# Ten modulation units of the first block's projection, multiplied and added on VectorE instead of on the array

## The chip, the cores and the metric

One core of a Trainium2 chip runs the whole kernel. The metric is the device time of one execution in microseconds (us). The engines are PE (TensorE, the matmul array; PEld is its weight load), DVE (VectorE), ACT (ScalarE), POOL (GpSimd) and SP, which issues the transfers. Each has its own instruction queue and goes through it in order. An engine waits for another by a semaphore, and whatever stands behind the waiting instruction in the same queue waits with it.

## The reference

A first block (a state-space scan, windowed attention, a mixture of experts) is followed by two layers of a second block. The change touches only how the modulation vectors are made while the first block's input is projected. They are one row times a matrix, for the latent tokens and for the context:

```python
mod_x = jax.nn.silu(c) @ w_ada[layer] + b_ada[layer]
mod_c = jax.nn.silu(c_ctx) @ w_ada[layer] + b_ada[layer]
sh1, sc1, g1, sh2, sc2, g2 = jnp.split(mod_x[:, None, :], 6, axis=-1)
...
hx = rms_norm(x, norm1[layer]) * (1 + sc1) + sh1
hc = rms_norm(ctx, norm1[layer]) * (1 + csc1) + csh1
zx, xbc_x, dt_x, qx, kx, vx = split_projection(hx @ w_in[layer])
zc, xbc_c, dt_c, qc, kc, vc = split_projection(hc @ w_in[layer])
```

`w_ada` has 1024 rows and 6 x 1024 columns, `c` and `c_ctx` are vectors of 1024, and all is float32. Inside the stretch looked at here the modulation only has to be ready for later phases; the projection itself does not read it.

## The kernel before

All weights come through one stream: units of 1024 rows by 256 columns (1 MB), loaded by SP in a fixed order into a ring of four slots (`weight_ring`). A slot is loaded again when the unit in it has been used. A matmul tells this: `retire()` marks the units held so far as used, and the next matmul that passes through `note()` carries the signal (`WeightStream`, line 75).

The first projection is `seven_phase` with the name `project1` (called at line 3357). It has nine weight units, numbered 0 to 8 here, and behind each stand two modulation units in the stream (`burst=2`), 18 in all, numbered 0 to 17. Modulation units 8 to 17 stand behind the last five weight units. A weight unit is a matrix product in seven block products instead of eight (a Strassen form): POOL makes four sums of the quarters of the weights (`weight_quarters`, 128x512 each, during the unit before), DVE has made the sums of the columns once at the start, PE makes seven products of four matmuls (128x256), ACT copies three of the results out of PSUM, POOL makes one small sum (`m15`), and DVE makes four sums, called here u2, c22, c12 and c21 by their semaphores. Units 0, 1, 2 and 8 also have context columns, 16 more matmuls ahead of the seven products. Behind the four sums of units 0 to 3 DVE also does the short convolution of that unit's output (`ShortConv.taps`).

A modulation unit has four steps, each with a counter of its own, all in class `Modulation` (line 290):

- `rows`, on PE at the end of a weight unit: eight matmuls (32 columns of `silu_c` against 128x256 of the weights), which leave partial rows in PSUM;
- `copy`, on ACT: those rows to SBUF;
- `turn`, on PE, behind the first and the second product of the next weight unit: two small matmuls that turn the rows into columns and add them;
- `add`, on DVE: the bias. It stands in DVE's queue behind the four sums of its unit, so ahead of the next unit's u2.

Two later phases, `gates` and `mlp`, use the other form, `SummedModulation` (line 370), with the same four steps and one more, `piece`, on DVE. There DVE multiplies the weights by the values of `silu_c`, one value for each partition, and adds the eight row blocks up in `mod_products`, once for the latent vector and once for the context's. A piece is four instructions of 128x256, so a modulation unit is four pieces, 16 instructions: two `tensor_scalar` (line 403) and 14 `scalar_tensor_tensor` (line 406). `rows` then waits until the unit's 16 instructions are done (line 421), and needs four matmuls of 128x128 that only add over the partitions. `turn` is one matmul. A unit named in `whole` takes the old form in every step.

PE's queue is the order of the calls in the Python loop: the products of unit i, then `rows` of its two modulation units, then unit i+1. DVE's queue in the same way: u2, c22, c12, c21, taps, two `add`, then unit i+1.

Of the kernel before, what the change touches and what calls it, by code (L numbers as in the profile page):

```python
# [2833 lines left out]
def seven_phase(core, name, b, lo, n, units, th=None, conv=None, mods=(), burst=0, heads=None, tail=None):  # L2834
# [6 lines left out]
    q = Quarters  # L2841
    U = len(units)
    with core.phase(name, U + len(mods)) as ph:
        bg = Modulation(core, ph, mods) if mods else None
        kq = KeyQuery(core, ph, *heads) if heads else None
        st = SquareTail(core, ph, *tail) if tail else None
        if th is None:
# [17 lines left out]
        def quarter(i, r, c):  # L2865
            return units[i][r][:, T - 2 * n + c * n:T - 2 * n + (c + 1) * n]
# [126 lines left out]
        def _(dve):  # L2993
            link = chain(dve, vec_link) if conv else None

            def plus(dst, bank, other, f):
                if f == 1.0:
                    return nc.vector.tensor_tensor(dst, bank, other, ALU.add)  # L2998
                return nc.vector.scalar_tensor_tensor(dst, bank, f, other, ALU.mult, ALU.add)

            column_quarters(nc.vector, b, lo, n, th, t_ready, False)
            for i in range(U):
# [7 lines left out]
                dve.wait_ge(products, 7 * i + 3)  # L3010
                dve.wait_ge(m1_out, i + 1)
                plus(quarter(i, 0, 1), y, quarter(i, 1, 0), f).then_inc(u2_out, 1)
                if kq and len(kq.turns.get(i, ())) == 2:
                    kq.sines(dve, stream.tables_loaded, i, 0)
                    kq.add(dve, i, 0)
                dve.wait_ge(products, 7 * i + 5)
                dve.wait_ge(m15_out, i + 1)
                plus(quarter(i, 1, 1), y, quarter(i, 1, 1), f).then_inc(c22_out, 1)
                if kq and len(kq.turns.get(i, ())) == 1:
                    kq.sines(dve, stream.tables_loaded, i, 0)  # L3020
                    kq.add(dve, i, 0)
                dve.wait_ge(products, 7 * i + 6)
                dve.wait_ge(u2_out, i + 1)
                plus(quarter(i, 0, 1), z, quarter(i, 0, 1), f).then_inc(c12_out, 1)
                dve.wait_ge(products, 7 * i + 7)
                plus(quarter(i, 1, 0), y, quarter(i, 1, 0), f).then_inc(c21_out, 1)
                if kq:
                    kq.sines(dve, stream.tables_loaded, i, 1)
                if conv and i < conv.pairs:
# [773 lines left out]
```

## Time and profile before

| | us |
|---|---|
| median of 3 runs | 4199.21 (4193.64 to 4199.97) |
| the profiled execution | 4195.06 |
| its span, first to last instruction | 4193.2 |
| PE busy | 3856.6 (92% of the span) |
| DVE busy | 1874.2 (45%) |
| POOL busy | 1031.2 (25%) |
| ACT busy | 873.3 (21%) |
| granted PE clock, mean | 0.967 of full |

The phase `project1` lies from 75.8 to 249.1 us of the span; its last five weight units run from 159.6 to 241.7 us. In the tables a busy share is a share of time in which the engine had an instruction under way; a matmul row of the timeline with "x8" is four matmuls of float32, each shown as two passes. The granted clock is 1.00 at 2.4 GHz and 0.50 at 1.2 GHz.

### The profile page before, as it was taken

The numbers are of one execution on the slowest core, as the hardware profiler recorded it, in microseconds if no ns is written. First come the engines' busy times: TensorE is split into PE (matmuls) and PEld (weight loads), VectorE is DVE, ScalarE is ACT, GpSimd is POOL, SyncE is SP. The second block draws the span as 40 slices with busy tenths as digits, with TensorE's granted clock in tenths as the row PEclk, the third lists the DMA queues.
The fourth block names the chain that finished last, engine by engine and source line by source line (L and its number), as shares of the span: only waits on it lengthen the run. The fifth ranks groups of instructions, "written<-read, shape, count | busy, mean of one in ns | idle before, by whom it ended". The sixth has DMA issues, their size and how long they took to land. (4 is left out here: it accounts for less than half of the span.)

```text
span 4193.2 us, 47533 instructions
## 1 busy us (share of the span) xinstructions
PE 3856.6 (92%) x18216; PEld 2581.9 (62%) x18216; DVE 1874.2 (45%) x3401; ACT 873.3 (21%) x1681; POOL 1031.2 (25%) x862
## 2 busy tenths in 40 slices
PE   6967969999989988999997999999899989989998
PEld 4865734444465566555554555555787657758887
DVE  3445332222322266588543666645225645234344
ACT  2122321111111265111213000001123511220001
POOL 1301200000014211223341322231142023434443
PEclk8978989999999999999998999999999999999999
DMA  5410159999811100122221223221110012222221
GB/s 197 171 73 16 49 237 390 394 395 395 340 36 50 46 11 1 62 91 98 76 98 40 101 101 121 101 91 51 45 61 31 1 67 83 74 81 72 90 82 60
DMA packets 72155, 479.61 MB, mean 114 GB/s; under 512 B 8256, under 2 KB 9664, under 8 KB 18176
## 3 DMA queue, kind: packets, MB, share of 16 engines
q1 hardware_dynamic: 68720, 465.86, 29.4%
q0 software_dynamic: 2640, 8.65, 0.7%
q8 instruction: 147, 2.41, 0.2%
q10 hardware_dynamic: 576, 2.10, 0.1%
q14 instruction: 72, 0.59, 0.0%
HBM read 472.39 MB, written 4.19 MB: 114 GB/s over the span
## 5 line engine op out<-in xcount | busy, mean ns | idle before, releaser
L2164 DVE SCALAR_TENSOR_TENSOR sb_x_all<-ps,sb_modulation_ada,sb_x_all 128x512 f32<-128x512 f32 x144 | 106.5, 750 | 323.4 <-PE ps L2001 302.9
L754 PE MATMUL ps<-projected,weight_ring 128*128 128x384 f32 (+1 forms) x672 | 245.8, 521 | 0.0
L754 PEld LDWEIGHTS ps<-projected,weight_ring 128*128 128x128 f32 x672 | 127.7, 190 | 106.1 <-issue 45.9
L3116 PE MATMUL ps<-h2b,weight_ring 128*128 128x384 f32 (+1 forms) x512 | 154.1, 445 | 23.6 <-PEq L246 23.6
L1151 DVE TENSOR_REDUCE attention_shift<-ps 128x1 f32<-128x768 f32 (+1 forms) x160 | 130.9, 845 | 74.8 <-PE ps L1039 74.3
L2554 DVE SCALAR_TENSOR_TENSOR projected<-projected,sb_vectors 128x497 f32<-128x497 f32 (+26 forms) x270 | 157.8, 649 | 1.6
L1039 PE MATMUL ps<-projected 64*128 64x256 f32 (+1 forms) x576 | 133.8, 519 | 24.9 <-DVE projected L1180 15.0
L406 DVE SCALAR_TENSOR_TENSOR mlp_mod_products<-weight_ring,sb_silu_c,mlp_mod_products 128x256 f32<-128x256 f32 x280 | 154.6, 622 | 0.1
L2414 PE MATMUL ps<-projected,gates_weight_sums 128*128 128x384 f32 (+1 forms) x512 | 149.6, 435 | 5.0 <-POOL gates_weight_sums L2694 5.0
L1837 POOL DMA_INDIRECT h<-tokens,own_tokens x31 | 31.1, 1002 | 491.2 <-PE ps L1972 416.4
L2414 PE MATMUL ps<-h2b,weight_ring 128*128 128x384 f32 (+1 forms) x512 | 150.1, 436 | 1.9 <-PEq L246 1.9
L2414 PE MATMUL ps<-h2b,gates_weight_sums 128*128 128x384 f32 (+1 forms) x512 | 149.7, 435 | 0.6 <-POOL gates_weight_sums L2691 0.4
L3095 POOL TENSOR_TENSOR mlp_weight_sums<-weight_ring 128x512 f32<-128x512 f32 x32 | 45.8, 1432 | 398.3 <-DMA weight_ring<-w_stream 315.2
L2998 DVE TENSOR_TENSOR projected<-ps,projected 128x384 f32<-128x384 f32 (+1 forms) x72 | 35.3, 490 | 233.7 <-PE ps L2903 233.7
L3116 PEld LDWEIGHTS ps<-h2b,weight_ring 128*128 128x128 f32 x512 | 98.3, 194 | 66.1 <-issue 29.4
L1988 PE MATMUL ps<-expert_weights,experts_x_turned 128*64 128x256 f32 x944 | 135.0, 384 | 1.9 <-DVE experts_x_turned L2156 1.9
L1112 ACT ACTIVATE attention_prob<-ps,attention_shift 128x768 f32<-128x768 f32 (+1 forms) x160 | 129.6, 813 | 34.1 <-DVE attention_shift L1151 33.2
L2394 POOL TENSOR_TENSOR merged<-merged,gates_sigmoid 128x768 f32<-128x768 f32 (+1 forms) x44 | 67.2, 1538 | 278.4 <-DVE gates_sigmoid L2620 278.4
L2001 PE MATMUL ps<-experts_slot_owner,experts_down_out_pair 128*128 128x512 f32 x240 | 134.0, 643 | 0.0
L796 PE MATMUL ps<-weight_ring,h2b 128*128 128x256 f32 (+1 forms) x576 | 108.6, 352 | 20.9 <-PEq L246 20.9
L2414 PEld LDWEIGHTS ps<-projected,gates_weight_sums 128*128 128x128 f32 x512 | 97.8, 191 | 47.2 <-POOL gates_weight_sums L2694 6.1
L2063 PE MATMUL ps<-expert_weights,experts_hidden_turned 128*64 128x512 f32 x528 | 120.6, 597 | 6.2 <-DMA expert_weights<-w_moe 3.4
(673 smaller groups left out, 8023.9 us busy)
## 6 DMA issues: line engine op xcount, KB each, us to landing
weight_ring<-w_stream SPq DMA_DIRECT2D x218, 1024.0 KB, 5.0
expert_weights<-w_moe SPq DMA_DIRECT2D x125, 1024.0 KB, 21.8
weight_ring<-w_moe SPq DMA_DIRECT2D x40, 1024.0 KB, 24.0
h2b<-w_moe SPq DMA_DIRECT2D x33, 1024.0 KB, 21.4
weight_ring<-w_stream SPq DMA_DIRECT2D x16, 512.0 KB, 3.6
weight_ring<-w_stream SPq DMA_DIRECT2D x16, 384.0 KB, 3.2
sb_x_all<-xT SPq DMA_DIRECT2D x1, 3072.0 KB, 11.7
tokens<-h_tokens ACTq DMA_DIRECT2D x4, 512.0 KB, 12.5
```

The lines of the kernel that those rows point to most:

```text
L406: ins = self.core.nc.vector.scalar_tensor_tensor(acc, w[:, k, :], c, acc, ALU.mult, ALU.add)
L754: ins = nc.tensor.matmul(core.ps[:, 2 * slot + half, 0:n], w_of(k), h_of(k)[:, a:a + n], start=(first and k == 0), stop=(last and k == chu ...
L796: ins = nc.tensor.matmul(core.ps[:, 2 * (j % 4), 0:n], h[:, k, t * P:(t + 1) * P], w[:, k, c:c + n], start=(k == 0), stop=(k == KD - 1))
L1039: ins = nc.tensor.matmul(scores(p, i)[:, at:at + n], q, k[:, c:c + n], start=True, stop=True, skip_group_check=True)
L1112: nc.scalar.activation(prob[:, b, 0:n], scores(p, i)[:, 0:n], ACT.Exp, bias=shift[:, b:b + 1], accum_out=sums[:, b:b + 1]).then_inc(p_read ...
L1151: nc.vector.tensor_reduce(shift[:, b:b + 1], scores(p, i)[:, 0:columns(p)], AX.X, ALU.max, negate=True).then_inc(peak_ready, 1)
L1988: ins = nc.tensor.matmul(out[OWN * j:OWN * (j + 1), :], x_t[:, k, :], w[j][:, k, :], start=(k == 0), stop=(k == KD - 1), skip_group_check= ...
L2001: nc.tensor.matmul(ps[:, bank, :], y_pair[:, m % 2, r, k % 4 * P:(k % 4 + 1) * P], owner[:, r, :], start=True, stop=True).then_inc(spread_ ...
L2063: ins = nc.tensor.matmul(down[OWN * r:OWN * (r + 1), :], hid_t[:, k % 2, OWN * (k // 2):OWN * (k // 2 + 1)], w[j][:, k, :], start=(k == 0) ...
L2414: ins = nc.tensor.matmul(acc, wq[:, k, :], bq[:, k, :], start=(first and k == 0), stop=(last and k == 3), skip_group_check=True)
L2554: ins = nc.vector.scalar_tensor_tensor(pr[:, acc + c, lo:hi], pr[:, val + c, lo + d:hi + d], w, pr[:, acc + c, lo:hi], ALU.mult, ALU.add)
L3116: ins = nc.tensor.matmul(acc, wq[:, k, :], bq[:, k, :], start=(first and k == 0), stop=(last and k == 3), skip_group_check=True)
```

## The change

In a `seven_phase` that has a convolution, which is `project1` alone, the modulation is of the summed form. `whole` is the first `burst * conv.pairs` = 8 modulation units, which keep the array form. Modulation units 8 to 17, behind weight units 4 to 8, are summed. Behind each of DVE's four sums stand two calls of `piece`; for the units in `whole` they only count. The other phases that call `seven_phase` are as before. The extra tile `mod_products` takes 4 KB of each partition.

```diff
-        bg = Modulation(core, ph, mods) if mods else None
+        summed = conv is not None
+        whole = range(burst * conv.pairs) if conv else ()
+        bg = SummedModulation(core, ph, mods, lambda i: i + i // burst + 1, whole) if summed else \
+            Modulation(core, ph, mods) if mods else None
...
                 plus(quarter(i, 0, 1), y, quarter(i, 1, 0), f).then_inc(u2_out, 1)
+                if summed:
+                    for _ in range(burst):
+                        bg.piece(dve)
...
                 plus(quarter(i, 1, 1), y, quarter(i, 1, 1), f).then_inc(c22_out, 1)
+                if summed:
+                    for _ in range(burst):
+                        bg.piece(dve)
...
                 plus(quarter(i, 0, 1), z, quarter(i, 0, 1), f).then_inc(c12_out, 1)
+                if summed:
+                    for _ in range(burst):
+                        bg.piece(dve)
...
                 plus(quarter(i, 1, 0), y, quarter(i, 1, 0), f).then_inc(c21_out, 1)
+                if summed:
+                    for _ in range(burst):
+                        bg.piece(dve)
```

What `bg` calls now for modulation units 8 to 17 (in the kernel before, used by other phases):

```python
    def piece(self, dve):
        n, q = divmod(self.n_piece, 4)
        ...
        if n in self.whole:
            return
        if q == 0 and n >= self.turns:
            dve.wait_ge(self.rows_done, n - self.turns + 1)
        w = self.core.stream.arrived(dve, self.place(n))
        ...
                if k == 0:
                    ins = self.core.nc.vector.tensor_scalar(acc, w[:, k, :], c, None, ALU.mult)
                else:
                    dve.wait_ge(self.multiplied, self.done_to(n) + 2 * k + s - 1)
                    ins = self.core.nc.vector.scalar_tensor_tensor(acc, w[:, k, :], c, acc, ALU.mult, ALU.add)

    def rows(self, pe):
        ...
        stream.take(pe)
        if n >= self.turns:
            pe.wait_ge(self.added, n - self.turns + 1)
        pe.wait_ge(self.multiplied, self.done_to(n + 1))
        stream.retire()
        for j in range(4):
            s, m = divmod(j, 2)
            ins = nc.tensor.matmul(self.bank(n)[32 * j:32 * j + 32, 0:P], self.core.first_of_32(),
                                   self.acc[:, n % self.turns, s, m * P:(m + 1) * P], start=True, stop=True,
                                   skip_group_check=True)
```

DVE's queue from the end of unit 3 to the first `add` of unit 5, before (`z_q` is written by the four sums, lines 364 and 464 are `add`):

```order
L1247 SCALAR_TENSOR_TENSOR conv_out<-conv_in,sb_vectors,conv_out 128x510 x2
L364 TENSOR_TENSOR sb_modulation_ada<-ps,sb_vectors 128x4 x2
L2998 TENSOR_TENSOR z_q<-ps,z_q 128x256 x4
L364 TENSOR_TENSOR sb_modulation_ada<-ps,sb_vectors 128x4 x2
L2998 TENSOR_TENSOR z_q<-ps,z_q 128x256 x4
```

The same place now (the line of the sum, 2998 before, is 3001):

```order
L364 TENSOR_TENSOR sb_modulation_ada<-ps,sb_vectors 128x4 x2
L3001 TENSOR_TENSOR z_q<-ps,z_q 128x256
L403 TENSOR_SCALAR project_mod_products<-weight_ring,sb_silu_c 128x256 x2
L406 SCALAR_TENSOR_TENSOR project_mod_products<-weight_ring,sb_silu_c,project_mod_products 128x256 x6
L3001 TENSOR_TENSOR z_q<-ps,z_q 128x256
L406 SCALAR_TENSOR_TENSOR project_mod_products<-weight_ring,sb_silu_c,project_mod_products 128x256 x8
L3001 TENSOR_TENSOR z_q<-ps,z_q 128x256
L403 TENSOR_SCALAR project_mod_products<-weight_ring,sb_silu_c 128x256 x2
L406 SCALAR_TENSOR_TENSOR project_mod_products<-weight_ring,sb_silu_c,project_mod_products 128x256 x6
L3001 TENSOR_TENSOR z_q<-ps,z_q 128x256
L406 SCALAR_TENSOR_TENSOR project_mod_products<-weight_ring,sb_silu_c,project_mod_products 128x256 x8
L464 TENSOR_TENSOR sb_modulation_ada<-ps,sb_vectors 128x4 x2
```

Thirty-two instructions have come in between a unit's sums and behind the last of them, eight after each.

PE's queue from the last product of unit 4 into unit 5, with the semaphores that are waited for, before:

```order
L2903 MATMUL ps<-mixed,weight_ring 128x256 x3
L317 MATMUL ps<-weight_ring,sb_silu_c 32x256 [waits project1_mod_added,unit_loaded2]
L317 MATMUL ps<-weight_ring,sb_silu_c 32x256 x7
L317 MATMUL ps<-weight_ring,sb_silu_c 32x256 [waits project1_mod_added,unit_loaded3]
L317 MATMUL ps<-weight_ring,sb_silu_c 32x256 x7
L2903 MATMUL ps<-h,weight_ring 128x256 [waits project1_c11_out,unit_loaded0]
```

and now:

```order
L2906 MATMUL ps<-mixed,weight_ring 128x256 x3
L423 MATMUL ps<-project_mod_products,sb_constants 32x128 [waits project1_mod_added,project1_mod_multiplied,unit_loaded2]
L423 MATMUL ps<-project_mod_products,sb_constants 32x128 x3
L423 MATMUL ps<-project_mod_products,sb_constants 32x128 [waits project1_mod_multiplied,project1_mod_added,unit_loaded3]
L423 MATMUL ps<-project_mod_products,sb_constants 32x128 x3
L2906 MATMUL ps<-h,weight_ring 128x256 [waits project1_c11_out,unit_loaded0]
```

The number of matmuls falls from 16 to 8, each of its two groups now also waits for DVE's counter of finished multiplications, and the next unit's first product stands behind both groups as it did.

## Rows read from the trace of the kernel before

**Rows 1.** Windows, all engines: us, length, busy (instructions) each, clock, DMA
```profile
174.60:189.70 15.10, 15.10 (x101) 12.42 (x97) 2.02 (x6) 1.92 (x5) 5.75 (x5) 1.00 0.55 211
...
219.70:243.00 23.30, 23.18 (x140) 19.51 (x136) 2.26 (x8) 3.72 (x9) 0.72 (x1) 1.00 0.38 147
```

**Rows 2.** Timeline of PE, units 6 to 8: start, length, what
```profile
189.67 1.99 PE L2903 MATMUL ps<-h,weight_ring 128*128 128x256 f32 x8
191.50 0.50 PE L341 MATMUL ps<-sb_constants,project_mod_rows 128*128 128x2 f32 x4
...
202.85 1.93 PE L317 MATMUL ps<-weight_ring,sb_silu_c 128*32 128x256 f32 x32
204.71 1.99 PE L2903 MATMUL ps<-h,weight_ring 128*128 128x256 f32 x8
...
219.76 7.17 PE L2913 MATMUL ps<-h,weight_ring 128*128 128x256 f32 x32
```

**Rows 3.** Timeline of DVE, the four sums of units 4, 6, 8
```profile
165.97 0.42 DVE L2998 TENSOR_TENSOR z_q<-ps,z_q 128x256 f32<-128x256 f32 x1 [0.21 <-PE ps L2903]
...
196.05 0.42 DVE L2999 SCALAR_TENSOR_TENSOR z_q<-ps,z_q 128x256 f32<-128x256 f32 x1 [1.67 <-PE ps L2903]
...
233.04 0.42 DVE L2998 TENSOR_TENSOR k_twice<-ps,k_twice 128x256 f32<-128x256 f32 x1 [1.67 <-PE ps L2903]
```

**Rows 4.** Timeline of ACT at the end of this phase
```profile
241.84 0.38 ACT L331 ACTIVATE project_mod_rows<-ps 128x256 f32<-128x256 f32 x1 [0.48 <-PE ps L317]
...
249.34 1.28 ACT L1312 ACT_TABLE_LOAD   x1 [0.26 <-PEq L246]
```

**Rows 5.** Timeline of DVE in the mlp phase, the pieces there
```profile
2406.68 0.61 DVE L403 TENSOR_SCALAR mlp_mod_products<-weight_ring,sb_silu_c 128x256 f32<-128x256 f32 x2
2407.21 4.48 DVE L406 SCALAR_TENSOR_TENSOR mlp_mod_products<-weight_ring,sb_silu_c,mlp_mod_products 128x256 f32<-128x256 f32 x6
...
2417.02 0.56 DVE L3236 TENSOR_TENSOR mlp_u<-ps,mlp_m 128x384 f32<-128x384 f32 x1 [2.02 <-PE ps L3116]
2417.49 3.25 DVE L406 SCALAR_TENSOR_TENSOR mlp_mod_products<-weight_ring,sb_silu_c,mlp_mod_products 128x256 f32<-128x256 f32 x8
2420.66 0.55 DVE L3251 TENSOR_TENSOR down<-mlp_u,mlp_m 128x384 f32<-128x384 f32 x1
```

**Rows 6.** Timeline of POOL in the mlp phase, same stretch
```profile
2408.60 1.39 POOL L3095 TENSOR_TENSOR mlp_weight_sums<-weight_ring 128x512 f32<-128x512 f32 x1 [15.69 <-DMA weight_ring<-w_stream]
2409.96 1.45 POOL L3096 TENSOR_TENSOR mlp_weight_sums<-weight_ring 128x512 f32<-128x512 f32 x1
```

**Rows 7.** Timeline of POOL, weight sums during unit 4
```profile
168.44 1.26 POOL L2691 TENSOR_TENSOR project_weight_sums<-weight_ring 128x512 f32<-128x512 f32 x1 [3.38 <-DMA weight_ring<-w_stream]
...
172.24 1.27 POOL L2696 TENSOR_TENSOR project_weight_sums<-weight_ring,project_weight_sums 128x512 f32<-128x512 f32 x1
```

**Rows 8.** DMA issues from 159.6 to 243 us
```profile
weight_ring<-w_stream SPq DMA_DIRECT2D x15, 1024.0 KB, 6.8
```

**Rows 9.** Timeline of PE in the mlp phase: the summed form
```profile
2403.24 0.43 PE L423 MATMUL ps<-mlp_mod_products,sb_constants 128*32 128x128 f32 x8
...
2406.28 0.28 PE L450 MATMUL ps<-sb_constants,mlp_mod_rows 128*128 128x4 f32 x2
```

**Rows 10.** Timeline of PE: work after three gaps
```profile
152.35 1.99 PE L2903 MATMUL ps<-mixed,project_weight_sums 128*128 128x256 f32 x8 [2.94 <-DVE conv_in L2998]
...
277.00 9.28 PE L1408 MATMUL ps<-state_x,b_tokens 128*128 128x256 f32 x32 [7.17 <-PEq L246]
...
309.65 0.69 PE L1491 MATMUL ps<-ssd_scan_segment,dt_x 128*64 128x128 f32 x2 [3.67 <-DVE ssd_scan_segment L1539]
```

**Rows 11.** Windows around those gaps, columns as in rows 1
```profile
149.40:152.40 3.00, 0.06 (x2) 0.05 (x1) 2.89 (x6) 0.39 (x1) 2.38 (x2) 1.00 0.00 0
277.00:280.90 3.90, 3.90 (x9) 3.17 (x10) 0.73 (x2) 0.00 (x0) 0.00 (x0) 0.50 0.02 4
...
309.70:315.00 5.30, 5.30 (x25) 5.30 (x26) 2.14 (x6) 1.12 (x2) 0.00 (x0) 0.50 0.02 3
```

## The prediction

> **What bounds the kernel now.** I read the windows of the last weight units first, then the timelines of PE and DVE there, then the phase that already has the summed form. The windows show PE busy for all of unit 5, 15.10 of 15.10 us, at the full clock, while DVE is busy 2.02 us and POOL 5.75 us; the window of unit 8 with what follows reads the same way, 23.18 of 23.30 us [rows 1]. So PE bounds this stretch, and work taken from it would shorten the kernel one for one, if nothing else came late. A unit without context takes 15.04 us (204.71 - 189.67), of which the two modulation units' array work is 1.86 us (204.71 - 202.85) [rows 2]. The one thing PE hands to others and gets back late enough to matter is small: the first of DVE's four sums starts 6.38 us into unit 6 (196.05 - 189.67) [rows 2, 3].
>
> **What the change takes from PE.** `rows` of a pair falls from 1.86 us to about 0.8: the summed form's group of one modulation unit is 0.43 us [rows 2, 9]. A `turn` falls from 0.50 to 0.28 us, 0.44 for two [rows 2, 9]. That is some 1.5 us a unit and 7.5 us over five units, if PE never had to wait.
>
> **What it gives to DVE.** Thirty-two instructions a unit. In the mlp phase eight multiply-adds in a row start 3.17 us before what follows them (2420.66 - 2417.49), 0.396 each, and two `tensor_scalar` take 0.53 (2407.21 - 2406.68) [rows 5]. A sum of 384 columns there holds the queue for 0.47 us (2417.49 - 2417.02) with a duration of 0.56; the sums here have 256 columns and a duration of 0.42, so I take 0.33 [rows 3, 5]. From the start of u2 to the last multiply-add's end: 4 x 0.33 + 2 x (0.53 + 6 x 0.396) + 2 x 3.17 + 0.08 for the last one's tail = 13.55 us, without any stall.
>
> **Why that lies on the path.** It cannot run beside the whole unit. u2 is ahead of every piece of its unit, and u2 needs the unit's third product; the first product in turn stands in PE's queue behind the second `rows` group of the unit before, which now waits for the last piece of that unit. And the queue of DVE has the two `add` ahead of u2, which wait for `turn` in the same new unit, so DVE cannot begin the next unit's pieces early either. The chain closes: start of the unit, three products and two turns, u2, eight pieces of four instructions, `rows`, next unit. Between u2 and the end of unit 6's products PE has only 202.85 - 196.05 = 6.8 us of work [rows 2, 3], and the pieces with the sums take twice that. What PE waits for last at the end of each of the five units is DVE.
>
> c22 comes later too, since two pieces, eight instructions, stand ahead of it, and the seventh product waits for it. That moves PE's work within the gap and costs nothing at the end. The first modulation unit's `rows` is ready after four pieces, in the gap as well.
>
> **Two surcharges.** First, POOL's four weight sums for the next unit. In the mlp phase the six multiply-adds that meet two of POOL's sums take 4.48 us where 6 x 0.396 + 0.08 = 2.46 are due, 1.0 us for each sum that they meet, and POOL's sums themselves take 1.39 and 1.45 us [rows 5, 6] where they take 1.26 and 1.27 alone [rows 7]. In unit 4 all four lie behind u2 (168.44 to 173.51, u2 at 165.97) [rows 3, 7], so 4.0 us. In units 5 to 7 the slot for the next weight unit comes free with the second `rows` group, its load is then alone, and the median of a load here, three at a time, is 6.8 us [rows 8]; POOL should start some 5 to 8 us into the unit, about when u2 does. I take 3.5 us, between 0 and the 4.0 of all four. Unit 8 has no unit behind it: 0.
>
> The Trainium skill (SBUF — State Buffer, Who interferes with whom) says that a VectorE instruction with two inputs in SBUF and a GpSimd instruction that reads SBUF exclude each other for a whole instruction, and the second to issue fully blocks. By that rule four sums of 1.27 us could hold DVE for 5.1 us instead of 3.5 to 4.0, and my sum would be up to 6 us longer. The rows above have 1.0 us each, and the sum goes by them.
>
> Second, PE's clock. PE will stand for some 6 us at the end of each of these units. After a gap of 2.94 us the clock is still 1.00, after 3.67 and 7.17 us work starts again at 0.50, and stays there for 5.3 and 3.9 us [rows 10, 11]. Half of that time is lost, 2.0 to 2.7 us, all of it ahead of u2. I take 2.2 us a unit for units 5 to 8; bounds 0 (no fall) and 5.9 (half speed all the way to u2 doubles the 5.94 us before it). Unit 4 starts with the clock full.
>
> The Trainium skill (TensorE: Matmul & The Clock Gate, HAM oscillation) describes this: a loop that leaves PE idle once in every round restarts cold in every round. By a rule that a warm PE stays warm the sum would be 8.8 us shorter; the gaps in this trace bear the page out.
>
> **The sum.** Unit 4, whose turns are still of the old form: 6.38 + 13.55 + 4.0 + 0.4 for the waking of PE and the second `rows` = 24.3, against 15.04: +9.3. Units 5 to 7: 6.38 - 0.44 = 5.94, + 2.2 + 13.55 + 3.5 + 0.4 = 25.6: +10.55 each, 31.7 for three. Unit 8 has context first: u2 starts at 13.28 (233.04 - 219.76), less 0.44, + 2.2 + 13.55 + 0.4 + 0.1 = 29.1 until ACT's last copy, which was at 241.84 - 219.76 = 22.08: +7.0 [rows 2 to 4]. ACT has the convolution's silu behind that copy and ends the phase, so the phase ends later by the whole shift: its next phase began at 249.34 [rows 4]. Nothing that follows waits for anything but this phase's end, so I let nothing of it come back.
>
> Sum: 9.3 + 31.7 + 7.0 = 48.0 us. The profiled execution took 4195.06 us, so 4243 us by it; it lies 4.15 us below the median of the runs, and against the median this is 4247 us, my forecast. What tells from no change here is 0.2%, 8.4 us.
>
> **The rivals.**
>
> The other side: DVE is hidden, PE bounds as before, and only the 7.5 us of saved array work count: 4192 us. For it: DVE is nearly empty here, 2.02 us of 15.10 [rows 1]. Against: the pieces start only behind the third product, and are 32. It decides where the 32 instructions and the four sums fit into 6.8 us: (6.8 - 4 x 0.33) / 32 = 0.17 us an instruction, against 0.396. Chance 2%.
>
> PE's clock does not fall in the gaps, since each has a small group of matmuls in it: the sum loses 4 x 2.2 = 8.8 us, 4238 us. For it: 2.94 us did no harm. Against: between the first group and the last piece lie four pieces and two sums, over 6 us. 11%.
>
> POOL does not hold DVE up, since its sums fall ahead of u2 (the load comes alone and early): 4.0 + 3 x 3.5 = 14.5 us less, 4233 us. It needs POOL to be through 6 us into the unit, and its load then must land before the unit begins. 7%. With both of these, 48.0 - 8.8 - 14.5 = 24.7 us are left: 4224 us, 2%.
>
> The clock stays low until u2 in every unit, the bound of 5.9 us: 4 x 3.7 = 14.8 us more, 4262 us. The longest stretch at 0.50 in the rows is 5.3 us, so this needs a worse restart than they show. 8%.
>
> That the change does not do what it says: the order of the queues shows the 160 instructions in place and 80 array matmuls replaced by 40. I give that nothing of its own.
>
> **How the numbers follow.** The forecast has 69%, with a range of its own of 4240 to 4254 us (clock 2.0 to 2.7 a unit, POOL 2.5 to 4.0). For 8 times in 10 I take 4231 to 4260: it takes in the case without POOL's delay, the one with the clock full, and most of the slow one. The first rival's 4192 lies 0.17% below the median, on the edge, so its 2% and 1% for what I have not thought of are split: faster by over 0.2% 1%, within 0.2% 2%. Slower: 97%.
>
> **What would show it.** Windows of units 4 to 8: PE busy about 13 us of a unit of 24 to 26 us, DVE about 18. PE's idle time there put down to DVE `project_mod_products`, some 6 to 8 us a unit, five times. The clock at 0.50 at the start of units 5 to 8 and at 1.00 when the unit's fifth product runs. DVE's multiply-adds at a start distance of 0.40 us, but three or four of some 1.45 us behind u2. The next phase's table load at about 297 us instead of 249.34. I am wrong if a unit stays at 15 us or less, if PE's wait is for a load or for POOL, or if a later phase changes by more than 3 us.

## The result, and the profile after

Before: 4196.43 us median of 4 runs beside the new ones (4191.75 to 4199.97). After: 4245.27 us median of 4 (4241.65 to 4248.90). The ratio is 1.0116, 95% interval 1.0102 to 1.0129: slower by 48.8 us, where 4247 was forecast.

The profiled execution of after took 4246.2 us, at a mean clock of 0.962 (0.967 before). Its page begins with these busy times. DVE had 1874.2 us in 3401 instructions before, so the 160 new ones are all there; PE had 3856.6 us, and is no less busy although it has less to do, since part of its work now runs at half the clock (the windows below show it):

```profile
span 4244.3 us, 47539 instructions
PE 3861.7 (91%) x18116; PEld 2586.9 (61%) x18116; DVE 1947.8 (46%) x3561; ACT 871.4 (21%) x1681; POOL 1031.1 (24%) x862
```

The windows of the five changed units, from one first product to the next, the last one up to ACT's last copy (columns as in [rows 1]), answer to the two windows there:

```profile
157.58:181.96 24.38, 14.53 (x85) 11.79 (x81) 23.33 (x46) 1.81 (x5) 6.26 (x5) 0.89 0.53 212
181.96:207.72 25.76, 16.58 (x81) 13.20 (x77) 16.92 (x38) 1.70 (x5) 5.84 (x5) 0.83 0.34 123
207.72:232.57 24.85, 15.66 (x81) 12.48 (x77) 16.93 (x38) 1.71 (x5) 5.85 (x5) 0.84 0.35 122
232.57:258.62 26.05, 16.87 (x81) 13.37 (x77) 16.92 (x38) 1.71 (x5) 5.85 (x5) 0.83 0.34 126
258.62:288.10 29.48, 22.85 (x114) 19.15 (x110) 13.96 (x38) 2.63 (x8) 0.72 (x1) 0.85 0.30 107
```

Units 4 to 7, which took 15.04 us, take 24.4 to 26.1. PE is busy for 14.5 to 16.9 us of it, DVE for 16.9 (23.3 in unit 4, which has the convolution too). The clock, 1.00 before, is 0.83 to 0.89 in the five windows. The timeline of PE through unit 5, answering to [rows 2] and [rows 9], shows where it stands:

```profile
181.37 0.65 PE L423 MATMUL ps<-project_mod_products,sb_constants 128*32 128x128 f32 x8 [6.30 <-DVE project_mod_products L406]
181.96 3.78 PE L2906 MATMUL ps<-h,weight_ring 128*128 128x256 f32 x8
...
185.82 2.58 PE L2906 MATMUL ps<-h,project_weight_sums 128*128 128x256 f32 x8
...
197.14 1.99 PE L2906 MATMUL ps<-mixed,weight_ring 128*128 128x256 f32 x8 [1.61 <-DVE z_q L3001]
200.40 0.42 PE L423 MATMUL ps<-project_mod_products,sb_constants 128*32 128x128 f32 x8 [1.26 <-DVE project_mod_products L406]
207.13 0.66 PE L423 MATMUL ps<-project_mod_products,sb_constants 128*32 128x128 f32 x8 [6.31 <-DVE project_mod_products L406]
207.72 3.58 PE L2906 MATMUL ps<-h,weight_ring 128*128 128x256 f32 x8
```

Three gaps: 1.61 us for c22, which stands behind the first eight instructions of DVE; 1.26 us for the first modulation unit's pieces; 6.31 us for the second's. Behind the long one the first product (x8) takes 3.78 us instead of 1.99, at a granted clock of 0.50 (181.96 to 185.80). The waits from 157 to 295 us put the summing matmuls' part down in one line (waited for: total, times, longest):

```profile
PE ps L423 <- DVE project_mod_products L406: 38.6, 10, 6.3
```

DVE through the same unit answers to [rows 3] and [rows 5], and POOL to [rows 6] and [rows 7]:

```profile
190.39 0.42 DVE L3001 TENSOR_TENSOR z_q<-ps,z_q 128x256 f32<-128x256 f32 x1 [1.67 <-PE ps L2906]
190.73 1.62 DVE L403 TENSOR_SCALAR project_mod_products<-weight_ring,sb_silu_c 128x256 f32<-128x256 f32 x2
192.27 4.48 DVE L406 SCALAR_TENSOR_TENSOR project_mod_products<-weight_ring,sb_silu_c,project_mod_products 128x256 f32<-128x256 f32 x6
196.67 0.41 DVE L3001 TENSOR_TENSOR z_q<-ps,z_q 128x256 f32<-128x256 f32 x1
197.01 3.24 DVE L406 SCALAR_TENSOR_TENSOR project_mod_products<-weight_ring,sb_silu_c,project_mod_products 128x256 f32<-128x256 f32 x8
...
203.74 3.25 DVE L406 SCALAR_TENSOR_TENSOR project_mod_products<-weight_ring,sb_silu_c,project_mod_products 128x256 f32<-128x256 f32 x8
```

```profile
189.65 1.27 POOL L2691 TENSOR_TENSOR project_weight_sums<-weight_ring 128x512 f32<-128x512 f32 x1
190.87 1.33 POOL L2692 TENSOR_TENSOR project_weight_sums<-weight_ring 128x512 f32<-128x512 f32 x1
192.16 1.32 POOL L2694 TENSOR_TENSOR project_weight_sums<-project_weight_sums,weight_ring 128x512 f32<-128x512 f32 x1
193.55 1.33 POOL L2696 TENSOR_TENSOR project_weight_sums<-weight_ring,project_weight_sums 128x512 f32<-128x512 f32 x1
```

DVE works without a pause from u2 at 190.39 to 206.99, and its first two groups, which lie beside POOL's last three sums, are long by about 3 us. ACT's end of the phase answers to [rows 4]:

```profile
287.83 0.28 ACT L439 ACTIVATE project_mod_rows<-ps 128x128 f32<-128x128 f32 x1 [6.68 <-PE ps L423]
...
295.22 1.28 ACT L1312 ACT_TABLE_LOAD   x1 [0.26 <-PEq L246]
```

I measure the phase from unit 4's first product to this load, so that small differences ahead of it don't count: 249.34 - 159.59 = 89.75 us before, 295.22 - 157.58 = 137.64 after, 47.9 us more. This is called the phase's shift below.

### The profile page after: what moved, and what is told of

Same layout as the page of the kernel before. It is cut to its first block and busy times, and to the rows that moved or that the text cites. A ratio compares the mean times of both kernels' runs of the same rounds, so it can differ in the third digit from the quotient of the medians.

```text
span 4244.3 us, 47539 instructions
## 1 busy us (share of the span) xinstructions
PE 3861.7 (91%) x18116; PEld 2586.9 (61%) x18116; DVE 1947.8 (46%) x3561; ACT 871.4 (21%) x1681; POOL 1031.1 (24%) x862
## 5 line engine op out<-in xcount | busy, mean ns | idle before, releaser
L754 PEld LDWEIGHTS ps<-projected,weight_ring 128*128 128x128 f32 x672 | 127.7, 190 | 106.1 <-issue 45.9
L1039 PE MATMUL ps<-projected 64*128 64x256 f32 (+1 forms) x576 | 134.5, 521 | 25.5 <-DVE projected L1180 15.1
L3131 PEld LDWEIGHTS ps<-h2b,weight_ring 128*128 128x128 f32 x512 | 98.1, 194 | 65.9 <-issue 29.1
## 6 DMA issues: line engine op xcount, KB each, us to landing
h2b<-w_moe SPq DMA_DIRECT2D x33, 1024.0 KB, 21.5
```

The lines of the kernel that those rows point to most:

```text
L754: ins = nc.tensor.matmul(core.ps[:, 2 * slot + half, 0:n], w_of(k), h_of(k)[:, a:a + n], start=(first and k == 0), stop=(last and k == chu ...
L1039: ins = nc.tensor.matmul(scores(p, i)[:, at:at + n], q, k[:, c:c + n], start=True, stop=True, skip_group_check=True)
L3131: ins = nc.tensor.matmul(acc, wq[:, k, :], bq[:, k, :], start=(first and k == 0), stop=(last and k == 3), skip_group_check=True)
```

## The experiments

All medians are of 4 to 11 runs, each beside runs of the kernel before on the same chip: 4194.85 us for the first four, 4194.5 for the next four, 4196.64 for the last two. "A unit" is unit 5, 6 or 7.

### What the shift is made of

Three kernels took one surcharge, the other, or both away. First POOL's: its four weight sums stay in the queue but work on 8 columns instead of 512, so that the products of these units are not the reference's (e5_pool):

```diff
-def weight_quarters(pool, s, w, ready, i):
+def weight_quarters(pool, s, w, ready, i, narrow=False):
...
+    if narrow:
+        for j in range(4):
+            pool.tensor_tensor(s[:, j, 0:1, 0:8], w[:, 0:1, 0:8], w[:, 4:5, 0:8], ALU.add).then_inc(ready, 1)
+        return
...
-                weight_quarters(pool, sw[:, i % 2], w, s_ready, i)
+                weight_quarters(pool, sw[:, i % 2], w, s_ready, i, conv is not None and i >= 5)
```

> The changed kernel, but POOL's four weight sums of units 5 to 8 work on 8 columns instead of 512, so these units' products are not the reference's. In the changed kernel's trace four of DVE's instructions in unit 4 and three in each of units 5 to 7 take about 1.0 us longer while POOL's sums run, 12.7 us together. Theory: these lie on the chain one for one, and the kernel is 12 to 14 us faster than the changed one, 36 us slower than before. Rival (the stalls are taken in a stretch that something else covers, or the clock's grid eats them): under 5 us faster than the changed one.

Measured: 4230.0 us, ratio 1.0083 [1.0069, 1.0097]; the phase's shift is 36.1 us, 11.8 less than in after. In DVE's timeline the same two groups are now short:

```profile
187.54 0.43 DVE L3005 TENSOR_TENSOR z_q<-ps,z_q 128x256 f32<-128x256 f32 x1 [1.67 <-PE ps L2910]
187.88 0.61 DVE L403 TENSOR_SCALAR project_mod_products<-weight_ring,sb_silu_c 128x256 f32<-128x256 f32 x2
188.40 2.46 DVE L406 SCALAR_TENSOR_TENSOR project_mod_products<-weight_ring,sb_silu_c,project_mod_products 128x256 f32<-128x256 f32 x6
```

The `tensor_scalar` pair goes from 1.62 to 0.61 us and the six multiply-adds from 4.48 to 2.46, one microsecond for each of three instructions. So POOL's sums cost 11.8 us in all; the gap of 6.31 us, which lies behind the collisions, is as it was.

With PE kept busy in the gap by 12 matmuls of no use (e6_filler):

```diff
+FILL = 12
...
-                for _ in range(burst):
+                for r in range(burst):
...
+                    if conv and 4 <= i < 8 and r == 0:
+                        pe.wait_ge(c11_out, i)
+                        for j in range(FILL):
+                            nc.tensor.matmul(banks(i + 1)[0], core.ones[:, :], b[:, 0, 0:256], start=True, stop=True,
+                                             skip_group_check=True)
```

> The changed kernel with 12 matmuls of 128x256 that nobody reads, put on PE behind the first of the two rows groups of units 4 to 7, some 5 us of work in a gap of 6.3. Theory: the clock stays full through the gaps, the three products ahead of u2 take 5.94 us again in units 5 to 8 instead of 7.5 to 8.7, and 8.6 us come back: 40 us slower than before. In the trace the granted clock is 1.00 at the start of units 5 to 8. Rival (the slow restart is not due to the gap, or the fillers run into the last piece and hold the next unit up): as slow as the changed kernel, 48 us, or slower.

Measured: 4231.55 us, ratio 1.0086 [1.0072, 1.0099]; shift 39.1 us, 8.8 less than in after. PE's timeline shows that the restart is at full speed (1.99 us for the first product, and a granted clock of 1.00 at the start of units 5 to 8) although DVE is no earlier:

```profile
198.96 0.43 PE L424 MATMUL ps<-project_mod_products,sb_constants 128*32 128x128 f32 x8 [1.26 <-DVE project_mod_products L407]
199.31 5.45 PE L2967 MATMUL ps<-h,sb_ones 128*128 128x256 f32 x24
205.69 0.43 PE L424 MATMUL ps<-project_mod_products,sb_constants 128*32 128x128 f32 x8 [0.93 <-DVE project_mod_products L407]
```

In unit 4 the clock fell all the same, behind a gap of 2.95 us and the first summing group. There the 12 matmuls themselves took 7.13 us instead of 5.45, at a mean clock of 0.76, and unit 5 began some 0.5 us later than in after:

```profile
175.59 7.13 PE L2967 MATMUL ps<-h,sb_ones 128*128 128x256 f32 x24
```

Both edits together (e7_both; the diffs are the two above):

> Both of these: POOL's weight sums of units 5 to 8 on 8 columns and the 12 matmuls in each gap. Theory: the two surcharges are separate and add up, 21.3 us less than the changed kernel, 27.5 us slower than before; what is left is 32 instructions of DVE a unit in the chain. Rival (they overlap, since what PE loses at the start moves POOL's sums off the pieces): less than 17 us less than the changed kernel.

Measured: 4221.42 us, ratio 1.0062 [1.0049, 1.0076]; shift 26.4 us, 21.5 less than in after, against 11.8 + 8.8 = 20.6 for the two alone. In the phase the surcharges add up. The medians bear this out only roughly: against the kernels before beside them the three lie 35.5, 37.1 and 26.9 us up, so 13.3, 11.8 and 21.9 less than after's 48.8. What is left, 26 us over five units, is that DVE's own run of 13.8 us stands where PE has 6.8 us of work.

Only the last unit's pair summed (e4_last), where neither POOL nor a next unit is behind it:

```diff
-        whole = range(burst * conv.pairs) if conv else ()
+        whole = range(16) if conv else ()
```

> The changed kernel with the first 16 modulation units in the array form, so that only the two behind unit 8 are summed. No POOL sums and a full clock there: 13.28 + 13.55 + 0.4 + 0.1 = 27.3 us to ACT's last copy against 22.08: 5.3 us slower than before. Rival (the loss of a unit is mostly a disturbance that a first summed unit starts, or lies in the changed start of the phase): under 2 us or over 9 us.

Measured: 4204.77 us, ratio 1.0026 [1.0015, 1.0037]; shift 5.7 us, where 5.3 was expected. The median lies 9.9 us above before's, which taken alone is the rival's figure (over 9). In the profile the rest, 3.8 us, comes up between this phase's end and the end of the experts' phase, in code that is the same. So the phase bears the theory out; what makes the rest is not shown.

### Is it the wait, or DVE's work as such?

The array does the rows as in the kernel before, DVE does the 160 instructions at the same places on other data, and PE waits for none of them (e1_nowait):

```diff
-        bg = SummedModulation(core, ph, mods, lambda i: i + i // burst + 1, whole) if summed else \
-            Modulation(core, ph, mods) if mods else None
+        bg = Modulation(core, ph, mods) if mods else None
...
+            def aside(dve):
...
+                            ins = nc.vector.tensor_scalar(acc, b[:, k, 0:UCOLS], c, None, ALU.mult)
...
+                            ins = nc.vector.scalar_tensor_tensor(acc, b[:, k, 0:UCOLS], c, acc, ALU.mult, ALU.add)
...
-                        bg.piece(dve)
+                        aside(dve)
```

> All 18 modulation units are of the array form again, and PE waits for no piece; DVE still does the same 160 multiply-adds in the same places, on columns of h instead of the ring's weights, into a tile that nobody reads. Theory (the loss is the closed chain: PE's rows wait for the last piece, and the next unit's u2 waits for PE): DVE then runs on its own at 13.55 + 0.2 + about 3.5 us for POOL = 17.2 us a unit against PE's 15.04, catches up in unit 8 where PE has 7 us of context work, and the kernel is 1 to 5 us slower than before, not 48. Rival (the pieces cost by being in DVE's queue, because u2 and c22 come late for PE's fifth and seventh product): 30 us or more slower.

Measured: 4206.33 us, ratio 1.0032 [1.0020, 1.0044]; shift 10.6 us. The theory is the nearer, 37 of 47.9 us go with the wait for the pieces, but both missed the size. The 10.6 us that stay are the rival's mechanism, u2 and c22 coming late, at a third of the size that it was given. With no wait to hold the units back, DVE needs more than a unit's time and its sums u2 and c22 come late; twice in unit 6 that stops PE:

```profile
198.37 1.89 PE L2922 MATMUL ps<-h,weight_ring 128*128 128x256 f32 x8
202.43 3.06 PE L2922 MATMUL ps<-mixed,project_weight_sums 128*128 128x256 f32 x8 [2.17 <-DVE z_q L3018]
205.29 2.55 PE L2922 MATMUL ps<-h,project_weight_sums 128*128 128x256 f32 x8
209.75 3.55 PE L2922 MATMUL ps<-mixed,weight_ring 128*128 128x256 f32 x8 [1.91 <-DVE z_q L3018]
```

Two gaps of about 2 us, 5 us apart, and the groups behind them take 3.06 and 3.55 us instead of 1.99: the clock fell here too. That unit took 23.0 us, units 4, 5 and 7 about 16.

### Is DVE too slow, or in the wrong place?

Half of the row blocks (e3_half), the others left out of the computation:

```diff
-            for s in range(2):
+            for s in range(2) if not (self.half and k % 2) else ():
...
```

> As the changed kernel, but only every second row block is multiplied and added, 8 instructions for a modulation unit instead of 16, so half of the sum is left out. Theory: a unit's chain loses 6.3 us. Unit 4: 6.38 + 7.2 + 3.5 + 0.4 = 17.5 us; units 5 to 7: 5.94 + 7.2 + 3.0 + 0.4 = 16.5 us if the clock holds in a gap of some 3 us, 18.7 if not; unit 8 about 1 us less than before. Together 6 us slower than before with the clock full, 13 with a fallen one. Rival (a cost for each unit that does not go with DVE's work, from waits and restarts): half of the loss of 48.8 us or more stays, 24 us slower.

Measured: 4214.44 us, ratio 1.0046 [1.0033, 1.0059]; shift 17.4 us. PE still waits 2.9 to 3.1 us for the last piece in units 4 to 7, and restarts on a lowered clock; I had expected 13 with the clock fallen, and the rival 24, so the median, 19.6 us up, meets neither. Unit 8, expected 1 us shorter than before, has 1.9 us of waiting for its last piece. Halving the work took 30 of the 48 us, not all.

Fourteen of the sixteen instructions of a modulation unit on 8 columns instead of 256 (e2_tiny), which leaves the rest of the columns out:

```diff
+                wk = w[:, k, :]
+                if self.narrow and k:
+                    acc, wk = acc[:, 0:8], w[:, k, 0:8]
...
-                    ins = self.core.nc.vector.scalar_tensor_tensor(acc, w[:, k, :], c, acc, ALU.mult, ALU.add)
+                    ins = self.core.nc.vector.scalar_tensor_tensor(acc, wk, c, acc, ALU.mult, ALU.add)
```

> As the changed kernel, but of each modulation unit's 16 instructions the 14 multiply-adds work on 8 columns instead of 256, so the modulation of these ten units is not computed. DVE then needs about 5 us a unit behind u2, under the 6.8 us that PE has there. Theory: PE never waits, and what is left is the saved array work, 1.5 us a unit, so 5 to 8 us less than before (about 4189). Rival (PE waits for something else that the new form brings, such as the ring's slots that are given back later, or the semaphores of 32 instructions): not faster than before.

Measured: 4224.25 us, ratio 1.0071 [1.0052, 1.0091], of which some 16 us arise in the experts' phase, whose routing hangs on the values: POOL gathers three of the extra blocks of tokens there (`experts_block_index`) instead of two. The phase itself is longer by 15.1 us. This missed by its sign: I had expected 5 to 8 us less than before. The two timelines of the same stretch, DVE's and then PE's, show why:

```profile
190.08 0.42 DVE L3006 TENSOR_TENSOR z_q<-ps,z_q 128x256 f32<-128x256 f32 x1
190.41 0.61 DVE L406 TENSOR_SCALAR project_mod_products<-weight_ring,sb_silu_c 128x256 f32<-128x256 f32 x2
190.94 0.96 DVE L409 SCALAR_TENSOR_TENSOR project_mod_products<-weight_ring,sb_silu_c,project_mod_products 128x8 f32<-128x8 f32 x6
191.82 0.42 DVE L3006 TENSOR_TENSOR z_q<-ps,z_q 128x256 f32<-128x256 f32 x1
192.15 1.23 DVE L409 SCALAR_TENSOR_TENSOR project_mod_products<-weight_ring,sb_silu_c,project_mod_products 128x8 f32<-128x8 f32 x8
```

```profile
189.06 2.00 PE L2911 MATMUL ps<-mixed,weight_ring 128*128 128x256 f32 x8 [0.38 <-DVE z_q L3006]
190.99 0.43 PE L426 MATMUL ps<-project_mod_products,sb_constants 128*32 128x128 f32 x8
193.53 0.54 PE L426 MATMUL ps<-project_mod_products,sb_constants 128*32 128x128 f32 x8 [2.11 <-DVE project_mod_products L409]
193.99 3.53 PE L2911 MATMUL ps<-h,weight_ring 128*128 128x256 f32 x8
```

The last eight instructions stand in DVE's queue behind c21 (191.82), and c21 waits for the unit's seventh product, whose matmuls end at about 191. However short they are, they come after PE has run out of products. Behind the 2.11 us of waiting the clock is down, 3.53 us for the next product. One unit later a wait of the same length left it at 1.00:

```profile
211.87 0.42 PE L426 MATMUL ps<-project_mod_products,sb_constants 128*32 128x128 f32 x8 [2.12 <-DVE project_mod_products L409]
212.23 2.00 PE L2911 MATMUL ps<-h,weight_ring 128*128 128x256 f32 x8
```

The place is not all of it, for the short instructions are short only away from POOL. Beside its sums six of them take three times as long:

```profile
185.69 2.98 DVE L409 SCALAR_TENSOR_TENSOR project_mod_products<-weight_ring,sb_silu_c,project_mod_products 128x8 f32<-128x8 f32 x6
```

That moves c22, c12 and c21 back as well. In unit 8, where POOL has no sums, PE waits 1.41 us for the last pieces; in units 4 to 7 it waits 2.1 to 2.8.

To test that it is the place, only the first row block was kept (e9_first): two `tensor_scalar` a modulation unit, those of the pair's second one behind c12, and nothing behind c21.

```diff
-        self.n_piece = 0
+        self.n_piece, self.per = 0, 16
...
-        return 16 * sum(i not in self.whole for i in range(n))
+        return self.per * sum(i not in self.whole for i in range(n))
...
-        for k in (2 * q, 2 * q + 1):
+        for k in (2 * q, 2 * q + 1) if self.per == 16 else (0,) if q == 0 else ():
...
+        if summed:
+            bg.per = 2
```

> Edit: of the eight row blocks of an image's modulation row only the first is multiplied (two tensor_scalar instructions a unit instead of two and fourteen multiply-adds); the other seven are left out, so the modulation of the layer is not computed, and the later phases, whose routing of tokens to experts hangs on it, may take another time. The phase alone is read: from unit 4's start to the next phase's table load. Theory (what is left of the cost in the two short-instruction runs is the place of the last pieces, not their speed: they stand behind the multilayer perceptron's c12 and c21 of the unit before, and any piece that is long past product 6 is late): one tensor_scalar of 0.26 us behind c12 is finished before TensorE's seventh product of 1.99 us ends, so TensorE waits for no piece, its clock stays at 1.00, and each of five units is shorter by the 1.5 us that TensorE no longer works: the table load comes 7 us earlier than in the kernel before, counted from unit 4's start (5 to 8). Rival (the rows of the modulation unit wait for something else as well, the transfer of the next unit or the rows of ScalarE): gaps of over 1 us before the second group of summing matmuls stay and the table load comes at the same time or up to 10 us later.

(Its c12 and c21 are those of this phase; no multilayer perceptron is near.) Measured: the phase is 6.3 us shorter than before (83.44 against 89.75), inside the 5 to 8 expected; PE waits for a piece 0.23 to 0.36 us in units 4 to 7, and the clock is 1.00 for the five units:

```profile
181.69 0.43 PE L423 MATMUL ps<-project_mod_products,sb_constants 128*32 128x128 f32 x8
182.35 0.43 PE L423 MATMUL ps<-project_mod_products,sb_constants 128*32 128x128 f32 x8 [0.23 <-DVE project_mod_products L403]
182.71 1.99 PE L2908 MATMUL ps<-h,weight_ring 128*128 128x256 f32 x8
```

(The whole kernel is at 4210.9 us, 1.0040 [1.0026, 1.0054]: the experts' phase again, some 19 us longer than before in the profile, with three gathered blocks instead of two as in e2_tiny.) So the array's saving is real, 7.5 us less the small waits, and in this order of the queues it is to be had only by work that is done before the seventh product ends. How much work that may be is not measured: this edit took away three things at once, the instructions behind c21, most of the work, and all but one of a unit's meetings with POOL's sums. That one makes the small wait: the second `tensor_scalar` behind c12 takes 1.36 us beside POOL.

### Can it be made to fit?

The first unit of each pair only, its pieces at the end of the unit before, behind u2 and behind c22 (e8_mix):

```diff
-        whole = range(burst * conv.pairs) if conv else ()
+        whole = [m for m in range(len(mods)) if m < burst * conv.pairs or m % 2] if conv else ()
...
+                if summed and 4 <= i < U - 1:
+                    for _ in range(2):
+                        bg.piece(dve)
...
```

> Only the first modulation unit of each pair behind units 4 to 8 is summed, and its four pieces stand earlier: two ahead of the two adds and u2 (in unit 4 behind u2), one behind u2, one behind c22. Its weights land 3.6 us into the unit. Theory: the last piece is done when the unit's products are, at about 13 us, and each of the five units saves 0.5 us in rows and 0.22 in one turn: 3 to 4 us faster than before, under what this measurement can tell from nothing, but PE's idle time in front of rows shows it in the trace. Rival (POOL's sums and the late u2 push the last piece behind the products): 1 to 3 us of wait in each unit, 4 to 12 us slower than before.

Measured: 4204.43 us, ratio 1.0021 [1.0012, 1.0030]; shift 9.2 us. The rival was right: PE waits for a piece 3.8 us in unit 4, 1.1 to 1.9 in units 5 to 7, and not at all in unit 8. Its timeline of DVE shows two things that I had not reckoned with:

```profile
186.02 4.07 DVE L406 SCALAR_TENSOR_TENSOR project_mod_products<-weight_ring,sb_silu_c,project_mod_products 128x256 f32<-128x256 f32 x4
...
195.44 0.62 DVE L403 TENSOR_SCALAR project_mod_products<-weight_ring,sb_silu_c 128x256 f32<-128x256 f32 x2 [4.68 <-DMA weight_ring<-w_stream]
```

The last four multiply-adds, 1.6 us alone, take 4.07 beside POOL's sums, and the early ones wait for their own weights' transfer. The version mended for both, with POOL's sums of units 6 to 8 held back until the pieces are done, and four modulation units summed instead of five (e10_fit):

```diff
-        whole = range(burst * conv.pairs) if conv else ()
+        whole = [m for m in range(len(mods)) if m < 10 or m % 2] if conv else ()
...
+                if summed and i >= 6:
+                    pool.wait_ge(bg.multiplied, 16 * (i - 5))
...
+                if summed and 4 <= i < U - 1:
+                    for _ in range(2):
+                        bg.piece(dve)
...
```

> Edit: only the modulation units behind units 5 to 8 that come first in their pair are summed (four of ten), their sixteen instructions stand in four pieces: two at the end of the unit before, one behind u2 and one behind c22, and GpSimd's weight sums of units 6 to 8 wait until that unit's pieces are done; the other six go through TensorE as in the kernel before. All of the computation is there. Theory: VectorE has 6.4 us of such work a unit, in places where it waits for TensorE now, no piece meets a weight sum of GpSimd, the last piece is finished some 1.5 us before TensorE's products end, and TensorE saves 0.72 us in each of four units: 4 x 0.72 = 2.9 us less than before, 4192, which is within what can't be told from no change; the phase is 3 us shorter in the profile and its clock stays at 1.00. Rival (VectorE's order has no free place at all: a piece moves c21, c22 or the weight sums that the next unit waits for): TensorE waits 1 to 2.5 us in each of the four units, and the time is 4 to 10 us longer than before.

Measured: 4194.97 us against 4196.64, ratio 0.9997 [0.9988, 1.0006]; the phase is 1.9 us shorter. The summing matmuls wait for nothing:

```profile
193.50 1.99 PE L2908 MATMUL ps<-mixed,project_weight_sums 128*128 128x256 f32 x8 [0.32 <-DVE z_q L3004]
...
198.88 0.43 PE L423 MATMUL ps<-project_mod_products,sb_constants 128*32 128x128 f32 x8
199.12 1.05 PE L317 MATMUL ps<-weight_ring,sb_silu_c 128*32 128x256 f32 x16
```

Most of the 2.9 us hoped for shows in the phase, the rest went to waits of 0.3 to 0.4 us for u2 in units 6 and 7, and none of it can be told from no change in the runs. Ahead of such a u2 one piece still meets a sum of POOL, the small `m15`, and its group takes 2.93 us instead of 2.46:

```profile
190.05 2.93 DVE L406 SCALAR_TENSOR_TENSOR project_mod_products<-weight_ring,sb_silu_c,project_mod_products 128x256 f32<-128x256 f32 x6
```

No version beat the kernel before.

## Why the prediction was right, step by step

**The chain.** Right. Each unit is the sum of three stretches that can be read from the rows above; for unit 5 they are 190.39 - 181.96 = 8.43 to u2, 206.99 - 190.39 = 16.60 of DVE, and 207.72 - 206.99 = 0.73 to the next unit, 25.76 in all. e5_pool's unit, without collisions, has DVE's run at 13.77 us, so 2.83 of the 16.60 are POOL's. The same reading of all five units, forecast beside measured:

| term, us | forecast | measured |
|---|---|---|
| clock, units 5 to 8 | 4 x 2.2 = 8.8 | 2.49, 1.57, 2.78, 1.73 = 8.6 |
| DVE from u2 to the last piece, alone | 13.55 | 13.77 (five times: +1.1) |
| POOL's surcharge, units 4 and 5 to 7 | 4.0 + 3 x 3.5 = 14.5 | 3.5 + 3 x 2.83 = 12.0 |
| from the last piece to the next unit or ACT's copy | 4 x 0.4 + 0.5 = 2.1 | 4 x 0.73 + 0.86 = 3.8 |
| unit 4, 5, 6, 7, 8 to the copy | 24.3, 25.6, 25.6, 25.6, 29.1 | 24.38, 25.76, 24.85, 26.05, 29.21 |
| shift of the phase | 48.0 | 47.9 |

That the shift is within 0.1 us is partly luck: three terms were off by +1.1, -2.5 and +1.7 us and cancel. The forecast of 4247 stood on a median before of 4199.21 us; beside the new runs it was 4196.43, and the two medians lie 48.8 us apart where the sum says 48.0. The range was wider than was said: the chances of the forecast, of the full clock and of POOL clear, which lie in 4231 to 4260, make 87% together, more than 8 in 10, before any of the slow case.

**POOL's surcharge** was mis-sized by 2.5 us. POOL's sums begin 7.7 us into unit 5 (189.65), 0.7 us ahead of u2, so three instructions of DVE met them and not three and a half; the price for each, 1.0 us, was right, and e5_pool measures the whole at 11.8. The page that I had weighed against it (the Trainium skill, SBUF — State Buffer, Who interferes with whom) would have made it up to 6 us more by a full exclusion; the rows decide for the smaller price. In unit 5 each of POOL's last three sums meets one instruction of DVE, which ends 0.15 to 0.28 us behind it, and POOL's sums are stretched as well, 1.33 us instead of 1.27.

**The clock.** Right, and e6_filler shows it as cause and not only beside it: DVE as late as before, PE busy, 8.8 us back. That the small group of matmuls before a long gap does not save the clock was argued in the prediction; all four restarts after a gap of 6.3 us came at half speed. That is what the Trainium skill tells of a loop that stands idle once a round (TensorE: Matmul & The Clock Gate, HAM oscillation): here every round restarted cold. With shorter gaps it did not hold for every round, as e2_tiny's two gaps of 2.1 us show.

**The wake and `rows`** was too small, 0.73 us for 0.4: the group itself runs at half the clock (0.65 us for 0.43), which I had priced as if warm. The other 0.1 us is not accounted for.

**The rivals.** Clock full would have been 4238 and POOL clear 4233; as experiments they gave 4231.55 and 4230.0, both together 4221.42 where the sum says 4224. These medians stand beside a kernel before of 4194.5 us, 4.7 less than the sum's; free of that, the phase's shifts are 39.1, 36.1 and 26.4 us where the sum has 39.2, 33.5 and 24.7. POOL's term, sized at 14.5 us and worth 11.8, is the one that was off. The first rival, DVE hidden, was rightly given 2%, but its point of decision was wrong. The prediction let it decide at 0.17 us an instruction; at 0.14 away from POOL's sums (e2_tiny) the phase was still 15.1 us longer. A price per instruction can't decide it, since a quarter of the instructions stand behind c21 and so behind the seventh product, and since the price is another beside POOL. The condition is one of place as well, and e9_first meets it.

**Later phases.** I had said that a change of over 3 us there would make me wrong. In the profile of after the next phase's table load is 45.9 us late and the end of the program 51.1, and 4.1 us of the difference come up in one stretch of 500 us behind the experts' phase, from the first matmul on `h2b` there to the first on `fourier_dft`. The same stretch is 3.3 to 3.6 us longer in e3_half, e5_pool and e6_filler, and within 0.2 us of before in e1_nowait, e7_both and e10_fit, with the same code in all of them. So I take it for scatter of single executions, not an effect of the pieces; the medians, 48.8 us apart where the phase's shift is 47.9, bear that out, and so do the profiled executions of e5_pool and e6_filler, which are the slowest of their five, 6.1 and 7.5 us above their medians. By the letter the sign of being wrong was there; the bound of 3 us was too tight for one profile. What sets the longer stretch is open.

## What to carry to other kernels

Before work is moved to an idle engine, find its place in that engine's queue: which wait stands ahead of it, and how much work the bounding engine still has from that wait to the point that needs the result. Here DVE was idle for 13 of 15 us, but the stretch from the first wait that counts to the end of PE's products was only 6.8 us, and behind the last wait there was none; the share of idle time said nothing. Add what the move collides with (here 1.0 us for each instruction that met one of POOL's weight sums) and what the new gap costs in clock (2.1 us a restart), since both came on top here and made 21 of the 48 us.

## What the runs showed of the hardware

- PE's clock is not told by the length of one gap. A lone gap of 2.94 us left it at 1.00 [rows 10, 11]; 2.11 us with a group of summing matmuls and a wait of 0.38 us ahead of it (e2_tiny), and gaps of 2.17 and 1.91 us some 5 us apart (e1_nowait), brought groups of 3.53, 3.06 and 3.55 us instead of 1.99. But one of 2.12 us in the next unit of e2_tiny, with a wait of 0.80 us ahead of it, left the product at 2.00 us and the clock at 1.00. What decides between the two is open here.
- The fall of the clock does not always cost the same: 1.57 to 2.78 us after four gaps of the same 6.3 us. Half speed lasted for different lengths: the first product takes 3.78, 3.58 and 3.78 us behind the first three, and the second 2.58, 1.97 and 2.87, where 1.97 is full speed.
- A multiply-add of 8 columns holds DVE for 0.14 us (eight of them 1.23 us) where one of 256 takes 0.40: a thirty-second of the columns, a third of the time. Beside POOL's weight sums the short ones lose as much as the long ones: 2.98 us for six instead of 0.96 (e2_tiny), 4.48 instead of 2.46 (after).
- A `tensor_scalar`, which reads one tensor only, is held up beside POOL as a multiply-add is: 1.62 us for two instead of 0.61. A sum that reads PSUM (`z_q<-ps,z_q`) is not: u2 of unit 5 takes 0.42 us under POOL's first weight sum, as it did alone.
